# Convolution feed-forward of a two-block transformer kernel: feature tiles as 512 plus 256 column products

## The reference

```
D_MODEL, SEQ, D_FF, CONV_WIDTH, DEPTH = 1024, 256, 2816, 3, 2

def rms_norm(x, gain):
    y = x * rsqrt(mean(x * x, axis=-1, keepdims=True) + EPS)
    return y * gain

def conv_ffn(x, w_up, conv_w, conv_b, w_down):
    h = x @ w_up                                  # (256, 1024) @ (1024, 5632)
    h = causal depthwise convolution of h over tokens, width 3, + conv_b
    gate, up = split(h, 2, axis=-1)
    return (silu(gate) * up) @ w_down             # (256, 2816) @ (2816, 1024)

for layer in range(DEPTH):
    h = h + mixer(rms_norm(h, attn_norm[layer]))  # HGRN2 in layer 0, sparse attention in layer 1
    h = h + conv_ffn(rms_norm(h, ffn_norm[layer]), ffn_w_up[layer], ffn_conv_w[layer],
                     ffn_conv_b[layer], ffn_w_down[layer])
```

## Time and profile before

| | us |
|---|---|
| median of 3 runs | 1654.92 |
| lowest, highest | 1654.91, 1657.29 |
| the profiled execution, its own time | 1655.93 |
| the span of its trace | 1654.1 |

### The profile page before, as it was taken

How to read it: one execution, slowest core, us unless ns; L and a number is a source line. 1 busy time by engine, 2 the same in 40 slices (tenths; PEclk the granted TensorE clock), 3 DMA queues, 4 the chain that set the end, 5 groups by cost and what they waited for, 6 DMA issues and landing times.

```text
span 1654.1 us, 30287 instructions
## 1 busy us (share of the span) xinstructions
PE 1621.6 (98%) x10649; PEld 1435.7 (87%) x10649; DVE 1200.8 (73%) x2072; ACT 951.6 (58%) x1612; POOL 71.0 (4%) x76
## 2 busy tenths in 40 slices
PE   7999999999999999999999999999999999999998
PEld 7888999988899997888879978888888889778887
DVE  5768877778677777766675977666866678676666
ACT  7465655565565556555576465555755557575554
POOL 5000000000000000000000000000090000000000
PEclk9999999999999999999999999999999999999999
DMA  9446666675356666766665556667566666336662
GB/s 266 141 128 194 200 189 182 182 153 128 100 180 184 185 185 197 229 190 189 191 198 162 180 174 208 189 188 193 162 202 190 189 179 176 105 119 205 189 188 87
DMA packets 393609, 292.68 MB, mean 177 GB/s; under 512 B 33419, under 2 KB 365476, under 8 KB 393152
## 3 DMA queue, kind: packets, MB, share of 16 engines
q1 hardware_dynamic: 390448, 280.83, 59.0%
q0 software_dynamic: 2944, 10.80, 1.9%
q10 hardware_dynamic: 144, 0.07, 0.0%
HBM read 290.59 MB, written 1.07 MB: 176 GB/s over the span
## 4 chain that ended last, share of the span: by engine, by line
PE 92%; DVE 5%; ACT 2%; issue 1%; DMA 0%; SPq 0%; DVEq 0%; ACTq 0%
PE ps L426 19%; PE ps L403 18%; PE ps L404 18%; PE ps L405 18%; PE ps L430 10%; DVE SQ L631 1%; PE ps L716 1%; DVE w_lo L394 1%; DVE H L637 1%; ACT w_hi L387 1%; PE ps L1037 1%; PE ps L513 0%; PE ps L461 0%; PE ps L462 0%; PE ps L2228 0%
## 5 line engine op out<-in xcount | busy, mean ns | idle before, releaser
L394 DVE TENSOR_TENSOR w_lo<-raw,w_hi 128x1024 fp32r<-128x1024 f32 x532 | 647.1, 1220 | 33.0 <-ACT w_hi L387 31.0
L387 ACT ACTIVATE w_hi<-raw 128x1024 fp32r<-128x1024 f32 x532 | 544.5, 1050 | 46.0 <-PE ps L405 31.1
L403 PE MATMUL ps<-x_both,w_hi 128*128 128x256 f32 x1224 | 350.6, 286 | 3.7 <-DVE x_both L563 1.8
L405 PE MATMUL ps<-x_both,w_hi 128*128 128x256 f32 x1224 | 346.2, 283 | 0.0
L404 PE MATMUL ps<-x_both,w_lo 128*128 128x256 f32 x1224 | 346.2, 283 | 0.0
L426 PE MATMUL ps<-x_both,w_hi 128*128 128x512 f32 x1360 | 339.7, 391 | 0.0
L426 PEld LDWEIGHTS ps<-x_both,w_hi 128*128 128x128 f32 x1360 | 249.5, 188 | 48.0
L403 PEld LDWEIGHTS ps<-x_both,w_hi 128*128 128x128 f32 x1224 | 234.4, 191 | 10.0 <-issue 5.1
L404 PEld LDWEIGHTS ps<-x_both,w_lo 128*128 128x128 f32 x1224 | 234.5, 192 | 1.7
L405 PEld LDWEIGHTS ps<-x_both,w_hi 128*128 128x128 f32 x1224 | 234.4, 192 | 0.0
L403 PE MATMUL ps<-w_hi,h_hi 128*128 128x512 f32 x536 | 210.7, 393 | 0.6 <-DVE h_lo L847 0.6
(11 more groups left out here) (333 smaller groups left out, 1871.3 us busy)
## 6 DMA issues: line engine op xcount, KB each, us to landing
raw<-in_ffn_w_up SPq DMA_DIRECT2D x176, 512.0 KB, 3.8
raw<-in_ffn_w_down SPq DMA_DIRECT2D x132, 512.0 KB, 4.5
raw<-in_ffn_w_gate SPq DMA_DIRECT2D x88, 512.0 KB, 4.6
raw<-in_hgrn_w_in SPq DMA_DIRECT2D x32, 512.0 KB, 5.4
raw<-in_gmlp_w_in SPq DMA_DIRECT2D x32, 512.0 KB, 4.4
raw<-in_gmlp_w_out SPq DMA_DIRECT2D x16, 512.0 KB, 3.7
raw<-in_hgrn_w_out SPq DMA_DIRECT2D x8, 512.0 KB, 3.5
raw<-in_dsa_w_in SPq DMA_DIRECT2D x16, 256.0 KB, 4.7
```

What stands on the lines that cost most here:

```text
L387: nc.scalar.activation(w_hi[:, s, :], raw[:, s, :], ACT.Copy).then_inc(hi_done, 1)
L394: nc.vector.tensor_tensor(w_lo[:, s, :], raw[:, s, :], w_hi[:, s, :].bitcast(F32), ALU.subtract)\
L403: pe.matmul(o, whi, xhi, start=first, stop=False, skip_group_check=not group)
L405: return pe.matmul(o, whi, xlo, start=False, stop=last, skip_group_check=not group)
```

## The change

All gate and up tiles of the convolution stages take the 512 plus 256 column form, but for the last up tile (tile 21), which stays as it is. For each changed tile ScalarE copies the second half of the bank into gs or us, and VectorE adds the first half to it in place. GpSimd, in the new function `conv_pool`, multiplies the sum by R in place. ScalarE's tap now waits for GpSimd (`conv_scaled`). `conv_pool` is called for both stages. It stands behind GpSimd's transfer of `toe` and a memset, and before the transfers of the gain rows.

```diff
@@ ffn_pe, up_part
-                    if conv:
-                        mm = feat_tile(pe, ps[:, 2 * par + what, 0:L], c + what, x_wait=xw)
+                    if conv and what and i0 == NF - 1:
+                        mm = feat_tile(pe, ps[:, 2 * par + what, 0:L], c + what)
                     else:
                         mm = feat_pair(pe, ps[:, 2 * par + what, :], c + what, x_wait=xw)
@@ ffn_act, it
+                act.wait_ge(used, c - HI_AHEAD + 1 + RING * n)
+                nc.scalar.activation(gs[:, par, :], ps[:, 2 * par, L:2 * L], ACT.Copy).then_inc(S("conv_half"), 1)
                 split_hi(act, c, n)
-                act.wait_ge(*tile("gate_read", f, i + 1))
+                act.wait_ge(*scaled(f, i, 0))
...
+                if i0 < NF - 1:
+                    act.wait_ge(used, c - HI_AHEAD + 2 + RING * n)
+                    if i0 > 0:
+                        act.wait_ge(S("conv_step"), 3 * i + 3 * NF * f)
+                    nc.scalar.activation(us[:, :], ps[:, 2 * par + 1, L:2 * L], ACT.Copy).then_inc(S("conv_half"), 1)
                 if i0 > 0:
                     high(i - 1, 1 - par)
...
-                act.wait_ge(*tile("up_read", f, i + 1))
+                if i0 < NF - 1:
+                    act.wait_ge(*scaled(f, i, 1))
+                else:
+                    act.wait_ge(*tile("up_read", f, i + 1))
@@ new
+        def conv_pool(pool, f):
+
+            pool.wait_ge(*once("r_done", FN[f]))
+
+            def scale(i, i0):
+                par = i0 % 2
+                pool.wait_ge(*tile("gate_read", f, i + 1))
+                nc.gpsimd.tensor_tensor(gs[:, par, :], gs[:, par, :], R[:, :], ALU.mult).then_inc(S("conv_scaled"), 1)
+                if i0 < NF - 1:
+                    pool.wait_ge(*tile("up_read", f, i + 1))
+                    nc.gpsimd.tensor_tensor(us[:, :], us[:, :], R[:, :], ALU.mult).then_inc(S("conv_scaled"), 1)
...
@@ conv_dve, it
-                gate_at = c + 1 + RING * n
-                dve.wait_ge(used, gate_at)
-                nc.vector.tensor_tensor(gs[:, par, :], ps[:, 2 * par, 0:L], R[:, :], ALU.mult).then_inc(S("gate_read"), 1)
+                dve.wait_ge(*halved(f, i, 0))
+                nc.vector.tensor_tensor(gs[:, par, :], ps[:, 2 * par, 0:L], gs[:, par, :], ALU.add).then_inc(S("gate_read"), 1)
...
-                dve.wait_ge(used, gate_at + 1)
-                nc.vector.tensor_tensor(us[:, :], ps[:, 2 * par + 1, 0:L], R[:, :], ALU.mult).then_inc(S("up_read"), 1)
+                if i0 < NF - 1:
+                    dve.wait_ge(*halved(f, i, 1))
+                    nc.vector.tensor_tensor(us[:, :], ps[:, 2 * par + 1, 0:L], us[:, :], ALU.add).then_inc(S("up_read"), 1)
```

More of the change, by code:

```diff
@@ L848, in low, with halved, scaled @@
                 .then_inc(S("hid_lo"), 1)
+        def halved(f, i, what):
+            return S("conv_half"), (2 * NF - 1) * f + 2 * i + 1 + what
+        def scaled(f, i, what):
+            return S("conv_scaled"), (2 * NF - 1) * f + 2 * i + 1 + what
+        def conv_pool(pool, f):
[7 more added lines that the diff above has]
+                    nc.gpsimd.tensor_tensor(us[:, :], us[:, :], R[:, :], ALU.mult).then_inc(S("conv_scaled"), 1)
+            for i in range(3):
+                scale(i, i)
+            with pool.Fori(1, 10) as n:
+                scale(2 * n + 1, 3)
+                scale(2 * n + 2, 4)
+            scale(21, 21)
         def conv_dve(dve, f):
@@ L898, in it @@
                     low(dve, f, i, 1 - par)
-                dve.wait_ge(used, gate_at + 1)
-                nc.vector.tensor_tensor(us[:, :], ps[:, 2 * par + 1, 0:L], R[:, :], ALU.mult).then_inc(S("up_read"), 1)
+                if i0 < NF - 1:
+                    dve.wait_ge(*halved(f, i, 1))
+                    nc.vector.tensor_tensor(us[:, :], ps[:, 2 * par + 1, 0:L], us[:, :], ALU.add).then_inc(S("up_read"), 1)
+                else:
+                    dve.wait_ge(used, c + 2 + RING * n)
+                    nc.vector.tensor_tensor(us[:, :], ps[:, 2 * par + 1, 0:L], R[:, :], ALU.mult).then_inc(S("up_read"), 1)
                 if 1 < i0 < NF - 1:
@@ L2412, in _ @@
             nc.gpsimd.memset(A[:, 8 * K1:8 * K1 + 260], 1.0).then_inc(S("ds_ones"), 1)
+            conv_pool(pool, 0)
             def gain(n, src):
@@ L2419, in _ @@
             gain("p2", T["ffn_post_g_2"][0, 0:1])
+            conv_pool(pool, 1)
             pool.wait_ge(*rows_of("ffn2", row_parts("ffn2")))
```

## The result

The changed kernel takes **1714.76 us** (median of 6 runs, 1711.1 to 1718.05) against 1655.53 for the kernel before in the same comparison. The ratio is 1.0356, with a 95% interval of 1.0345 to 1.0367. The profiled execution has a span of 1711.9 us, 57.8 more than before's 1654.1.

The account below looks back on a forecast made before the run. TensorE was taken to bound the kernel, at 8.50 us a pass; with GpSimd's multiply a pass becomes 9.6: 8.1 + 19.8 + 0.6 = 28.5 us a stage, 57 for both, forecast 1712 us, range 1674 to 1763.

Parts of the forecast that it names:

- TensorE's saving: Convolution feed-forward tiles: 0.095 us less a tile, a TensorE-bound pass from 8.50 to 8.31 us, 8.2 us for both stages.
- The multiply: GpSimd's in-place multiply by R, 256 columns: 0.18 us fixed plus 2 x 256 x 0.82 ns, 0.60 us.
- The ring: Steady pass from one ScalarE gate-tile copy to the next, through VectorE and GpSimd: closes at 9.6 us, above TensorE's 8.31.
- Waiting both ways: GpSimd's multiply waits for VectorE's two-SBUF-input instructions and then holds VectorE in turn; a pass of 9.6 us, chance 0.38.
- the power of the earlier trace: GpSimd's 42.07 us TENSOR_TENSOR (L2435) in the profile before; 16 w_lo beside it took 1218 ns in the median, as ever.
- Comes in between two VectorE instructions: GpSimd gets through between VectorE instructions: 1.10 us after a w_lo started, while VectorE would start its next at 1.14.
- the starved rival: GpSimd gets through only when VectorE stands or reads PSUM: a pass of 10.4 us, 1747 us; chance 0.25.
- Hidden: GpSimd's multiply is not held up at all and TensorE stays the bound at 8.31 us: 1647.5 us; chance 0.15.
- waits but does not hold: GpSimd waits for VectorE, VectorE never for GpSimd: a pass of 9.0 us, 1686 us; chance 0.17.
- The point from which the hidden case turns: Multiply with its waits: under 1.0 us TensorE stays the bound, at 1.2 us even with before, beyond that slower.
- The ends of a stage: First two passes 7.6 us each, the third 9.6, 8.1 more in all; last w_lo and h_lo 0.6 later.

Follow-up runs that it names:

- TensorE's part alone: Kernel before with 43 of 44 tiles per stage as 512 plus 256 columns, the second half of the bank dropped: 1649.9 us, ratio 0.9962.
- taking w_hi out: Changed kernel with ScalarE's third w_hi of a pass moved ahead of the up tap, all arithmetic kept: 1676.19 us, ratio 1.0131.
- the reordered run: Changed kernel with ScalarE's third w_hi ahead of the up tap and VectorE's add of the up tile ahead of the second w_lo: 1676.26 us, ratio 1.0117.
- one column: Changed kernel with both GpSimd multiplies cut from 256 columns to one: 1666.27 us, ratio 1.0056.
- the add one step earlier: Changed kernel with ScalarE's third w_hi ahead of the up tap and VectorE's up-tile add ahead of the second gate tap: 1658.22 us, ratio 1.0016.

## Why the prediction was right

**TensorE's saving** was put at 0.19 us a pass and at most 8.2 us in all. The run with TensorE's part alone has the pass of 8.31. Between the gate tiles 0 and 21 it is 3.9 us shorter a stage, 7.9 in both, and 6.1 us by the medians. The other 1.8 us don't lie in the stages. Beside before's trace, this one has 0.6 us more ahead of the first stage, 1.6 less between the stages and 2.8 more behind the second, which is no more than the scatter shown below.

**The multiply** was priced at 0.60 us and took 0.73. The fixed part was right (0.18 against 0.19), the columns were not: 2.13 ns against 2 x 0.82. It stayed within the bound of 0.8 us. The 0.56 us estimated from the Trainium skill (GPSIMD Engine Reference, Performance versus the Vector engine) is low too.

**The ring** came out at 9.57 where it was laid at 9.58, and the links say how much of this is luck. From the copy's start at 300.23, the up add is at 5.79 (5.88 in the forecast), because VectorE is held 0.54 in place of 0.60 and the add follows the copy 0.03 sooner. The hold is what the columns take (256 x 2.13 ns = 0.54 us). The fixed part passes while VectorE still works. From the third w_lo's start to the end of the multiply, 306.35 to 308.16, are 1.81 us in place of 1.74: it gets through 1.08 us after that start in place of 1.14, and then takes 0.13 more. The two sums, 0.09 us too long and 0.07 too short, nearly cancel, and that is luck. The largest single error is the 0.13 us. The links themselves were tried: taking w_hi out took 0.95 off, halving the multiplies 0.55.

**Waiting both ways** was the step with the most doubt, and it decided. What the changed profile should show was "multiplies of gs about 1.0 us and of us 1.7 us": they last 0.90 and 1.65, and the w_lo behind the first up tap 1.76. TensorE's wait for w_lo, put at about 1.3 us a pass, is 1.0. The Trainium skill (SBUF — State Buffer, SBUF: two separate sides) has the shared pair locked for a whole instruction, and the engine that comes second fully blocked. For these products the trace agrees that each waits for the other, 0.54 us of VectorE and 0.9 of GpSimd. It doesn't agree for the power of the earlier trace rows, beside which VectorE ran on, nor for the reordered run, where the multiply that was there first was passed over twice.

**"Comes in between two VectorE instructions"** was right at the two places that the changed kernel has, and too general as a sentence. Behind the third w_lo VectorE has nothing to do, so that place couldn't tell. Behind the first up tap it could, and there the starved rival (10.4 us, 1747) was refuted. In another order the same multiply starved, 3.11 us. The chance of 0.25 that I gave the rival was not too high.

**Hidden** and **waits but does not hold** fell by the 0.9 us and the 0.54 us of the same rows. The point from which the hidden case turns, a multiply of 1.2 us with its waits, fits: 1.65 was slower, and 1.10 with one column (pass 8.48) was even in the loop and lost 0.6% elsewhere. The point holds for this order alone: with the add one step earlier a multiply of 2.38 us left the pass at 8.31.

**The ends of a stage.** The first three passes came out at 7.06, 7.56 and 9.42, where I had 7.6, 7.6 and 9.6. The first was 0.5 shorter, and two things that I had left out work against each other in it. Pass 0 has no up taps, no product and no h_lo yet, and its first w_lo isn't held, 2.0 us less on VectorE. But w_lo stands right behind the gate add there, so the gate multiply waits for it to end, and VectorE then waits 1.27 us for the gate tap:

```profile
162.09 1.22 DVE L394 TENSOR_TENSOR w_lo<-raw,w_hi 128x1024 fp32r<-128x1024 f32 x1
...
162.32 1.58 POOL L875 TENSOR_TENSOR gs<-gs,R 128x256 f32<-128x256 f32 x1 [7.25 <-DVE gs L920]
...
164.57 1.00 DVE L900 SCALAR_TENSOR_TENSOR ga<-gs,vec,ga 128x255 f32<-128x255 f32 x2 [1.27 <-ACT ga L808]
```

The multiply ends 1.81 us after the w_lo started (162.09 to 163.90), exactly like the up multiply of the steady loop. The end of the stage was right, 0.54 against 0.6.

**What the prediction left out** is 3.5 us outside these parts. TensorE's rows at the end of the second stage, and the windows over them (stretch, its length, then for each engine busy time and count, the granted clock, the share of the DMA and GB/s):

```profile
684.57 0.39 PE L405 MATMUL ps<-w_lo,h_hi 128*128 128x512 f32 x1
688.93 0.76 PE L403 MATMUL ps<-w_hi,h_hi 128*128 128x512 f32 x1 [3.97 <-DVE h_lo L857]
...
690.34 0.63 PE L403 MATMUL ps<-w_hi,h_hi 128*128 128x512 f32 x1
690.77 0.63 PE L404 MATMUL ps<-w_hi,h_lo 128*128 128x512 f32 x1
...
694.73 0.40 PE L405 MATMUL ps<-w_lo,h_hi 128*128 128x512 f32 x1
694.97 0.39 PE L403 MATMUL ps<-w_hi,h_hi 128*128 128x512 f32 x1
```

```profile
690.00:694.00 4.00, 4.00 (x11) 3.13 (x10) 2.74 (x5) 3.33 (x5) 0.00 (x0) 0.50 0.40 120
694.00:698.00 4.00, 3.19 (x13) 2.24 (x12) 2.74 (x4) 2.56 (x6) 0.00 (x0) 0.95 0.37 131
```

After 3.97 us of standing still the matmuls start 0.43 us apart, and the granted clock of 690 to 694 is 0.50, the lower level of 1.2 GHz. From 694.5 they are 0.23 apart again. Twelve intervals at 0.2 us more are some 2.4 us of TensorE's time. Before has a dip of its own a little later (granted clock 0.79 from 641 to 649), so that not all of it is lost. From the last h_lo to the residual's first matmul (L513) it is 8.0 us against 6.5 before, and 4.1 against 3.4 in the first stage, where six intervals were slow. These two are 2.2 us. The remaining 1.3 us are 1.6 less between the stages and 3.0 more behind the second. Both are scatter. In the 13 traces, whose programs are the same in these stretches, the one between the stages takes 116.3, 117.9 or 119.3 us (granted clock 1.00, 0.99 and 0.97, in the eight traces read for it), and the one behind the second takes either 1008.6 to 1009.1 or 1011.6 to 1012.0, whatever the kernel does in the stages.

## What to carry to other kernels

A helper engine that does "only" an elementwise step costs its own length, its wait for the shared port and the hold that it puts on the other engine, and in the changed kernel all three lay in a ring that closes over several engines. So before moving work to an idle engine, lay one iteration end to end from a copy to the next copy, and see whether that ring, not any engine's busy share, is below the bound. And where the first and last iterations of a loop are bound by another engine than the middle, change only the middle: that alone turned no gain into 0.4%.

## What the runs showed of the hardware

- A GpSimd multiply of two float32 operands on 128 partitions takes 0.19 us and 2.13 ns a column (0.189, 0.461 and 0.733 us for 1, 128 and 256), 2.2 times VectorE's 0.34 us from start to start at 256 columns. The first of each stage takes 0.67 us more than the later ones, whatever its columns (1.58 against 0.90, 1.30 against 0.63, 1.03 against 0.36). That is no start-up cost: it is issued beside a w_lo, where the later ones are issued beside a tap, and with the w_lo ahead of the tap in every pass all of them take 1.6.
- Beside VectorE's instructions with two SBUF inputs it is let in at some boundaries and not at others. Let in: between the first up tap and w_lo, and between w_lo and the first up tap. Passed over: between w_lo and h_lo (twice), and between the second gate tap and w_lo. Between h_lo and w_lo it was let in in one kernel and passed over in another. Each kernel did the same in every pass of its steady loop (up multiply 2.38 to 2.40 us in one, 3.11 to 3.13 in the other), so it isn't chance, but neither the operation ahead nor the length of the gap explains all of them. What decides stays open. I also have no run that shows why the power of 42 us held nobody.
- TensorE's granted clock was 0.50, the lower level, after a wait of 4.0 us at each stage's end, for 2.7 us in the first stage and 5.3 in the second.
